# Two row blocks of the first norm's modulation sums weighted on ScalarE and added on TensorE

## The chip, the cores and the metric

The kernel runs on one core of one Trainium2 chip. TensorE multiplies matrices into PSUM, VectorE and ScalarE do element-wise work, GpSimd (POOL) helps, and DMA queues carry data from HBM to SBUF. The metric is device time in microseconds (us) of one execution, start to end, lower is better. Three unprofiled runs of the kernel before took 1736.28, 1736.1 and 1733.9 us, median 1736.1.

## The reference

Two transformer-like blocks on 512 tokens of width 1024. What bears on this change is the very start of the first block: a conditioning vector `c` is turned into six vectors of 1024, two of which (`sh1`, `sc1`) shift and scale the first normalised input, before the first projection.

```
mod = jax.nn.silu(c) @ w_ada[l] + b_ada[l]
sh1, sc1, g1, sh2, sc2, g2 = jnp.split(mod, 6, axis=-1)
h = rms_norm(x, g_mix_norm[l]) * (1.0 + sc1[:, None]) + sh1[:, None]
proj = h @ w_in[l]
q_lat, kv_lat, k_pe, qd, kd, vd = jnp.split(proj, SPLITS, axis=-1)
```

So no product with `w_in` can start before some columns of `sc1` and `sh1` are known, and these need 2048 columns of `w_ada` (8 MB in fp32), each a sum over 1024 rows.

## The kernel before, in words

All engines run programs of their own, written out by hand, and meet at semaphores; there is no scheduler. The order of instructions on an engine is the order in the code.

The first norm works in four rounds r = 0 to 3. A round gives the shift and scale of 256 of the 1024 features, which are two of the eight feature tiles k (128 features each) that the projection sums over. Its parts:

- SP loads `w_ada` in 16 blocks of 512 KB into `adab` (`ada_block`, L769), four to a round: block u = 4r + 2 half + kind, kind 0 the scale and 1 the shift columns, half the first or second four of the eight row blocks of 128 rows. Between them SP loads the first weights (`stage`, L714).
- VectorE forms `acol` = sum over the eight row blocks k of silu(c)[k] * w_ada block k, a tile of 128 partitions by 512 (2 kinds by 256 columns): `column(r, k)`, one multiplication (L2287) and seven multiply-adds (L2289, the last of them L2291, which counts up `acol_done`). `columns(r, k0, k1)` runs a stretch of them; two are placed early and six later.
- TensorE adds `acol` over its partitions in `block_sums(r)`: four fp32 matmuls (two records each in the trace, x8) of a 128x128 weight tile with one column of ones (L1616), into four columns of PSUM bank 4.
- VectorE's `modulation(r)` (L2303, L2305) turns them into `gsc` and `mod`.
- ScalarE's `z_first(r)` scales and shifts two tiles of x in PSUM into `zu` and `zhi` (L1022, L1024), VectorE takes the rest as `zlo` (`z_low_first`, L2351). `zhi` + `zlo` is a split of an fp32 number for two fast passes.
- TensorE's `scaled_turn(k)` (L1520) transposes x tile k and scales its rows, and `first_products(k, jobs)` (L1627) multiplies tile k with the first four weight tiles: three matmuls of 512 columns for each job. From L1484 on the later projections follow.
- The weights are split in the same way: ScalarE's `split_hi` (`whi`, L919) and VectorE's `split_lo` (`wlo`, L2214).

TensorE's order is: scaled_turn 0, 1; transposes of the parameters (L1532) and of the meta tokens (L1536); block_sums(0); scaled_turn(2); products of tiles 0 and 1 with jobs 0, 1; scaled_turn(3); block_sums(1); scaled_turn(4); products of tiles 0 and 1 with job 2; scaled_turn(5); block_sums(2); products of tiles 2 and 3 with jobs 0 to 2; scaled_turn 6, 7; products of tiles 0 to 3 with job 3; block_sums(3); the rest of the products.

Of the kernel before, what the change touches and what calls it, by code (L numbers as in the profile page):

```python
# [8 lines left out]
ACT = mybir.ActivationFunctionType  # L9
# [4 lines left out]
P = 128  # L14
D = 1024
KD = D // P
# [194 lines left out]
def emit(nc, A, out):  # L211
# [4 lines left out]
    with ctx:  # L216
        def sem(name):
            return ctx.enter_context(nc.semaphore(name))
# [5 lines left out]
        def at(name, shape, off, dt=F32):  # L224
            n = 4 * int(np.prod(shape[1:]))
            assert base + off + n <= end, (name, base + off + n - end)
            return nc.alloc_sbuf_tensor_at(name, shape, dt, offset=base + off)

        cst = at("cst", [P, NCONST], 0)
        o = 4 * NCONST  # L230
# [3 lines left out]
        csil = at("csil", [P, 8], o + 2368)  # L234
# [14 lines left out]
        SQO = o  # L249
# [18 lines left out]
        adab = at("adab", [P, NADA, 4, 256], FREE + 16384)  # L268
# [12 lines left out]
        TAB = LAT + 24576  # L281
        tab = at("tab", [P, 4, T1], TAB)
        acol = [at(f"acol{i}", [P, 2, 256], TAB + 8192 + 2048 * i) for i in range(2)]
        posi = at("posi", [P, T1], TAB + 12288, I32)
        posf = at("posf", [P, T1], TAB + 14336)
        angt = at("angt", [P, 2, T1], TAB + 8192)
# [81 lines left out]
        ps = ctx.enter_context(nc.psum_tensor("ps", [P, 8, 512], F32))  # L368

        def const(name, rows=P, n=P):  # L370
            return cst[0:rows, CONST[name]:CONST[name] + n]
# [35 lines left out]
        s_xin, s_cst, s_par, s_meta = sem("s_xin"), sem("s_cst"), sem("s_par"), sem("s_meta")  # L407
        bulk_in = [sem(f"bulk_in{i}") for i in range(8)]
        s_cst2, s_pos, s_c, acol_done = sem("s_cst2"), sem("s_pos"), sem("s_c"), sem("acol_done")
        act_setup, dve_setup = sem("act_setup"), sem("dve_setup")  # L410
        rows_in = sem("rows_in")
        wide_in = [s_cst, s_cst2]
        ring_in = [sem(f"ring_in{i}") for i in range(RING)]
# [4 lines left out]
        ada_done, mod_mm, conv_mid = sem("ada_done"), sem("mod_mm"), sem("conv_mid")  # L418
# [187 lines left out]
        SUM_STEPS = [t for t in range(HEADS // 2 * QB, NS) if t % QB >= 2]  # L606

        FIRST_BANK = (0, 2, 1, 3)
        XN_AT = (2, 3, 6, 7, 8, 9, 10, 11)

        def xn(k):
# [298 lines left out]
        def _(act):  # L910
            link = Chain(act, a_link)

            def split_hi(u, i=None, step=4):

                slot, value = plan.landed[plan.w_load[u]]
                act.wait_ge(landed[slot], plus(value, i, 16 * step // NST))
                if u >= NHL:
                    act.wait_ge(marks, plus(plan.free[u - NHL], i, step))
                act.activation(whi[u % NHL][:], stage[slot][:], ACT.Copy).then_inc(hi_done, 1)  # L919
# [58 lines left out]
            for name, src, k in PARAMS:  # L978
                flat = A[src].rearrange("a b c -> (a b c)" if len(A[src].shape) == 3 else
                                        "a b -> (a b)" if len(A[src].shape) == 2 else "a -> a")  # L980
                v, r0, done = flat.rearrange("(r c) -> r c", c=P), ROW[name], 0
# [4 lines left out]
                    done += m  # L986

            act.wait_ge(start_mm, 1)
            act.activation(csil[:, :], ps[:, 2, 0:KD], ACT.Silu).then_inc(act_setup, 1)
            act.wait_ge(pads, 1)  # L990
            act.wait_ge(s_xin, 16 * QB)
            for t in range(QB):
# [2 lines left out]
            for k in (6, 7):  # L995
                act.wait_ge(xt_done, 6)
                act.wait_ge(xt_mm, k + 1)
                act.activation(xT[:, k, META:T2], ps[:, 5 + k % 2, :], ACT.Copy).then_inc(xt_done, 1)
            split_hi(0)
            split_hi(1)  # L1000

# [12 lines left out]
            def z_first(r):  # L1014

                act.wait_ge(dve_setup, 4 + r)
                for k in (2 * r, 2 * r + 1):
                    if k < 6:
                        act.wait_ge(start_mm, XN_AT[k])
                        if k >= NZU:  # L1020
                            act.wait_ge(zlo_done, k - NZU + 1)
                        act.activation(zu[:, k % NZU, 0:T1], xn(k), ACT.Identity, scale=gsc[:, 0, k:k + 1],  # L1022
                                       bias=mod[:, k:k + 1])
                        act.activation(zhi[:, k, 0:T1], xn(k), ACT.Identity, scale=gsc[:, 0, k:k + 1],  # L1024
                                       bias=mod[:, k:k + 1]).then_inc(zhi_done, 1)
                    else:
                        act.wait_ge(zu_done, 4 * (k - 5))
                        act.activation(zhi[:, k, 0:T1], zu[:, k % NZU, 0:T1], ACT.Copy).then_inc(zhi_done, 1)

            z_first(0)  # L1030
            split_hi(2)
            z_first(1)
            split_hi(3)
            z_first(2)
            z_first(3)

            def raw(name, j, split=True):
# [377 lines left out]
            for j in range(8):  # L1415
                ahead("glu", j)
                if j % 2:
                    for h in (j - 1, j):
                        act.wait_ge(ostat_mm, h + 1)
                        act.activation(wide(KH[:, h, :], T2), ps[:, 4 + 2 * (h % 2):6 + 2 * (h % 2), 0:HT2], ACT.Ln,  # L1420
                                       scale=1.0 / P, bias=small[:, 0:1]).then_inc(oln_done, 1)
                n = J["glu"] + j
# [35 lines left out]
            for h in range(2):  # L1458
                act.wait_ge(stat_mm, STAT0[6] + h + 1)
                r = small[:, 48 + 2 * h:50 + 2 * h]  # L1460
# [10 lines left out]
        def _(pe):  # L1471
# [35 lines left out]
            for k in range(KD):  # L1507
                if k >= 2:
                    pe.wait_ge(xt_done, k - 1)
                for t in range(QB):  # L1510
                    mm = pe.transpose(ps[:, 5 + k % 2, t * P:(t + 1) * P], xrow[:, t, k * P:(k + 1) * P], const("ident"))
                mm.then_inc(xt_mm, 1)
            def scaled_turn(k):

                if k == 2:
                    pe.wait_ge(dve_setup, 3)
                elif k > 2:
                    pe.wait_ge(zhi_done, k - 2)
                for t in range(QB):
                    mm = pe.matmul(ps[:, 5 + k % 3, t * P:(t + 1) * P], xrow[:, t, k * P:(k + 1) * P], diag[:, t, :],  # L1520
                                   start=True, stop=True)
                mm.then_inc(start_mm, 1)

            pe.wait_ge(dve_setup, 1)
            pe.wait_ge(xt_done, KD)
            scaled_turn(0)
            scaled_turn(1)
            pe.wait_ge(s_par, 16 * n_par)
            pe.wait_ge(s_par2, 16 * n_par2)
            for b in range(NBLK):  # L1530
                r = min(P, NROWS - b * P)
                mm = pe.transpose(ps[:, 1, b * P:b * P + r], prow[0:r, b, :], const("ident", r, r))  # L1532
            mm.then_inc(start_mm, 1)
            pe.wait_ge(s_meta, 16)
            for k in range(KD):
                mm = pe.transpose(ps[:, 7, k * META:(k + 1) * META], metar[:, k * P:(k + 1) * P],  # L1536
                                  const("ident", META, META))
# [67 lines left out]
                            if (h, k) == (1, KD - 1):  # L1605
                                mm.then_inc(marks, 1)

            def block_sums(r):

                if r:  # L1610
                    pe.wait_ge(dve_setup, 3 + r)
                pe.wait_ge(acol_done, r + 1)
                for i in range(2):
                    for kind in range(2):
                        c = 4 * r + 2 * i + kind
                        mm = pe.matmul(ps[:, 4, c:c + 1], acol[r % 2][:, kind, i * P:(i + 1) * P],  # L1616
                                       const("ones", n=1), start=True, stop=True)
                mm.then_inc(mod_mm, 1)

            def first_products(k, jobs):  # L1620

                pe.wait_ge(zlo_done, k + 1)
                for j in jobs:
                    if k == 0:
                        pe.wait_ge(split_done, j + 1)
                    for a, x in ((whi, zhi), (whi, zlo), (wlo, zhi)):
                        mm = pe.matmul(ps[:, FIRST_BANK[j], :], a[j][:, k * P:(k + 1) * P], x[:, k, 0:T1],  # L1627
                                       start=(k == 0 and a is whi and x is zhi), stop=(k == KD - 1 and a is wlo))
                    if k == KD - 1:
                        mm.then_inc(marks, 1)  # L1630
# [2 lines left out]
            scaled_turn(2)  # L1633
            first_products(0, (0, 1))
            first_products(1, (0, 1))
            scaled_turn(3)
            block_sums(1)
            scaled_turn(4)
            first_products(0, (2,))
            first_products(1, (2,))  # L1640
            scaled_turn(5)
            block_sums(2)
            first_products(2, (0, 1, 2))
            first_products(3, (0, 1, 2))
# [1 line left out]
            scaled_turn(7)  # L1646
            for k in range(4):
                first_products(k, (3,))
            block_sums(3)
            for k in range(4, KD):  # L1650
                first_products(k, (0, 1, 2))
# [530 lines left out]
            for j in range(8):  # L2182
                gemm("glu", j, zx(zhi), zx(zlo), T2, fresh=(ylo_done, 0) if j == 0 else None)
                if j % 2 == 0:
                    for h in (j, j + 1):
# [7 lines left out]
                        for b, t0, t1 in halves(T2):  # L2193
                            mm = pe.matmul(ps[:, 4 + 2 * (h % 2) + b, 0:HT2], const("ones"), KH[:, h, t0:t1],
                                           start=True, stop=True)
# [12 lines left out]
        def _(dve):  # L2208
# [68 lines left out]
            def column(r, k):  # L2277

                u = 4 * r + 2 * (k // 4)
                o, w, c = acol[r % 2][:, :, :], adab[:, u:u + 2, k % 4, :], csil[:, k:k + 1]  # L2280
                if k % 4 == 0:
                    for v in (u, u + 1):
                        dve.wait_ge(bulk_in[v % 8], 16 * (v // 8 + 1))
                if k == 0:
                    if r >= 2:
                        dve.wait_ge(mod_mm, r - 1)
                    link(dve.tensor_scalar(o, w, c, None, ALU.mult))  # L2287
                elif k < KD - 1:
                    link(dve.scalar_tensor_tensor(out=o, in0=w, scalar=c, in1=o, op0=ALU.mult, op1=ALU.add))  # L2289
                else:  # L2290
                    dve.scalar_tensor_tensor(out=o, in0=w, scalar=c, in1=o, op0=ALU.mult, op1=ALU.add).then_inc(acol_done, 1)  # L2291
# [16 lines left out]
                    else:  # L2308
                        ins.then_inc(dve_setup, 1)

            dve.wait_ge(act_setup, 1)
            for k in range(6):
                dve.wait_ge(xt_mm, k + 1)
                dve.tensor_copy(xT[:, k, META:T2], ps[:, 5 + k % 2, :]).then_inc(xt_done, 1)
# [668 lines left out]
            for j in range(8):  # L2983
# [15 lines left out]
                n = J["sp"] + j  # L2999
# [268 lines left out]
```

## Time and profile before

| what | us |
|---|---|
| median of three runs | 1736.1 |
| the profiled execution | 1734.03 |
| its span, first to last instruction | 1732.2 |
| TensorE busy | 1682.1 (97%) |
| VectorE busy | 1100.9 (64%) |
| ScalarE busy | 748.2 (43%) |
| GpSimd busy | 301.2 (17%) |

The 1.8 us between the profiled execution's time and its span lie before the first and behind the last instruction. Busy time is the sum of an engine's instruction records. Matmul ends are modelled and overlap the next start, so starts of matmuls are the better measure of pace. PEclk is the granted share of TensorE's full clock: 1.00 is 2.4 GHz, 0.50 is 1.2 GHz. The first norm lies in the first 60 us of the span. In the kernel after, line numbers differ by 2 to 35.

### The profile page before, as it was taken

How to read it: one execution, taken by the hardware profiler on the slowest of the kernel's cores; microseconds unless marked ns; L12 is line 12 of the kernel's file. 1: busy time of each engine (PE TensorE's matmuls, PEld its weight loads, DVE VectorE, ACT ScalarE, POOL GpSimd, SP SyncE). 2: the span in 40 equal slices, each digit the busy share in tenths (PEclk: the TensorE clock that was granted, in tenths of full speed). 3: DMA queues.
4: the chain of work that ended last, by engine and by line, in shares of the span. 5: the costliest groups of instructions: out<-in, count | busy, mean ns of one | idle time of the engine just before them, and what ended most of it. 6: DMA issues, size and time to landing. Idle time of an engine off the chain costs nothing.

```text
span 1732.2 us, 32425 instructions
## 1 busy us (share of the span) xinstructions
PE 1682.1 (97%) x12801; PEld 1493.0 (86%) x12801; DVE 1100.9 (64%) x1761; ACT 748.2 (43%) x1115; POOL 301.2 (17%) x289
## 2 busy tenths in 40 slices
PE   5999999999999999899999999999999999999998
PEld 4776666888888888799999999999999999989986
DVE  6877586777764668855869663444653766655633
ACT  4479574555332342632323554356233643323313
POOL 2112395211000003441015221110102000000002
PEclk8999999999999999999999999999999999999999
DMA  9453632343333232264336952242532233232332
GB/s 314 124 141 103 183 111 89 107 115 103 99 96 98 85 97 75 88 166 133 119 107 171 226 135 94 82 130 86 167 111 86 74 97 98 87 101 80 97 97 74
DMA packets 320398, 201.17 MB, mean 116 GB/s; under 512 B 50511, under 2 KB 303046, under 8 KB 320150
## 3 DMA queue, kind: packets, MB, share of 16 engines
q1 hardware_dynamic: 300208, 160.79, 33.2%
q0 software_dynamic: 7952, 24.83, 4.7%
q10 hardware_dynamic: 12118, 13.88, 2.3%
q8 instruction: 85, 1.39, 0.3%
q14 instruction: 35, 0.29, 0.1%
HBM read 177.75 MB, written 17.24 MB: 113 GB/s over the span
## 4 chain that ended last, share of the span: by engine, by line
PE 80%; DVE 9%; ACT 5%; issue 2%; DMA 2%; SPq 1%; POOL 1%; ACTq 0%; DVEq 0%
PE ps L1484 66%; DVE wlo L2214 2%; PE ps L1799 1%; PE ps L1686 1%; PE ps L1809 1%; PE ps L1825 1%; ACT whi L919 1%; PE ps L1627 1%; DMA stage<-in_w_in_dram 1%; PE ps L1603 1%; DVE acol L2289 1%; PE ps L2057 1%; PE ps L2151 1%; DVE LF L2876 1%; DMA xrow<-in_x_dram 1%
## 5 line engine op out<-in xcount | busy, mean ns | idle before, releaser
L1484 PE MATMUL ps<-zhi,whi 128*128 128x258 f32 (+2 forms) x2072 | 638.1, 308 | 1.4 <-ACT ub L1217 0.6
L1484 PE MATMUL ps<-zlo,whi 128*128 128x258 f32 (+2 forms) x2072 | 633.5, 306 | 0.0
L1484 PE MATMUL ps<-zhi,wlo 128*128 128x258 f32 (+2 forms) x2072 | 632.1, 305 | 0.0
L1484 PEld LDWEIGHTS ps<-zhi,whi 128*128 128x128 f32 x2072 | 390.9, 189 | 27.1 <-issue 3.9
L2214 DVE TENSOR_TENSOR wlo<-stage,whi 128x1024 fp32r<-128x1024 f32 x256 | 329.4, 1288 | 126.9 <-ACT whi L919 114.9
L1484 PEld LDWEIGHTS ps<-zlo,whi 128*128 128x128 f32 x2072 | 390.1, 188 | 19.0 <-issue 0.5
L1484 PEld LDWEIGHTS ps<-zhi,wlo 128*128 128x128 f32 x2072 | 390.8, 189 | 18.0
L919 ACT ACTIVATE whi<-stage 128x1024 fp32r<-128x1024 f32 x256 | 269.3, 1054 | 293.2 <-PE ps L1484 242.0
L1484 PE MATMUL ps<-ghi,whi 128*128 128x512 f32 x340 | 134.7, 396 | 0.0
L1484 PE MATMUL ps<-glo,whi 128*128 128x512 f32 x340 | 134.3, 395 | 0.0
L1484 PE MATMUL ps<-ghi,wlo 128*128 128x512 f32 x340 | 134.0, 394 | 0.0
L1217 ACT ACTIVATE ub<-ps 128x512 f32<-128x512 f32 (+1 forms) x88 | 52.6, 598 | 163.0 <-PE ps L1484 161.7
L3101 POOL TENSOR_TENSOR zu<-zu,sq 128x528 f32<-128x528 f32 (+1 forms) x18 | 31.7, 1761 | 425.5 <-ACT sq L927 424.6
L2629 DVE TENSOR_SCALAR cv<-ub,par 128x512 f32<-128x512 f32 (+1 forms) x88 | 49.0, 557 | 70.4 <-ACT ub L1217 70.4
L1227 ACT ACTIVATE ghi<-cv 128x512 f32 (+1 forms) x44 | 27.9, 634 | 124.3 <-DVE cv L2644 124.3
L1484 PEld LDWEIGHTS ps<-ghi,wlo 128*128 128x128 f32 x340 | 64.0, 188 | 15.0
L1484 PEld LDWEIGHTS ps<-ghi,whi 128*128 128x128 f32 x340 | 63.9, 188 | 14.7
L1484 PEld LDWEIGHTS ps<-glo,whi 128*128 128x128 f32 x340 | 63.9, 188 | 14.6
L2545 DVE TENSOR_TENSOR xT<-ps,xT 128x512 f32 (+2 forms) x30 | 20.8, 692 | 85.1 <-PE ps L1484 85.1
L2638 DVE SCALAR_TENSOR_TENSOR cv<-ub,par,cv 128x512 f32<-128x512 f32 (+1 forms) x88 | 66.3, 754 | 13.1 <-DVE cv L2632 6.7
L3094 POOL TENSOR_SCALAR pb<-pb,small 128x128 f32<-128x128 f32 (+3 forms) x64 | 72.8, 1156 | 9.6 <-DVE small L2519 9.2
L1274 ACT ACTIVATE spill<-ps 128x516 f32<-128x516 f32 (+1 forms) x40 | 24.2, 604 | 102.3 <-PE ps L1484 102.2
(449 smaller groups left out, 2806.0 us busy)
## 6 DMA issues: line engine op xcount, KB each, us to landing
stage<-in_w_up_dram SPq DMA_DIRECT2D x88, 512.0 KB, 3.8
stage<-in_w_in_dram SPq DMA_DIRECT2D x74, 512.0 KB, 4.0
stage<-in_w_down_dram SPq DMA_DIRECT2D x32, 512.0 KB, 4.0
ring<-in_w_ada_dram POOLq DMA_DIRECT2D x24, 512.0 KB, 4.5
adab<-in_w_ada_dram SPq DMA_DIRECT2D x16, 512.0 KB, 7.9
stage<-in_w_down_dram SPq DMA_DIRECT2D x16, 384.0 KB, 3.4
stage<-in_w_o_dram SPq DMA_DIRECT2D x8, 512.0 KB, 4.1
ring<-in_w_ada_dram SPq DMA_DIRECT2D x8, 512.0 KB, 3.9
```

The source lines that it names most:

```text
L919: act.activation(whi[u % NHL][:], stage[slot][:], ACT.Copy).then_inc(hi_done, 1)
L1217: act.activation(wide(ub[:, j % 2, 2:2 + T], T), acc(job, T), ACT.Copy).then_inc(emptied[job % 2], 1)
L1227: act.activation(ghi[c % 2][:, bass.ds(i * 2 + q, 1), 0:T].rearrange("p a t -> p (a t)"), cv[:, q, 1, 0:T], ACT.Copy).then_inc(ghi_done, 1)
L1274: act.activation(wide(spill[m % 2][:, T2 - T:T2], T), acc(n, T), fn).then_inc(emptied[n % 2], 1)
L1484: last = pe.matmul(out, w(a, k), x(k, t0, t1), start=(k == 0 and a is whi and x is x_hi), stop=(k == ks - 1 and a is wlo))
L1603: mm = pe.matmul(o, a[(u + j) % NHL][:, k * P:(k + 1) * P], x[:, k, c], start=(k == 0 and a is whi and x is zhi), stop=(k == KD - 1 and a ...
L2214: dve.tensor_tensor(wlo[u % NHL][:], stage[plan.w_load[u] % NST][:], whi[u % NHL][:].bitcast(F32), ALU.subtract).then_inc(split_done, 1)
L2545: ins = dve.tensor_tensor(x, acc(job, T), x, ALU.add)
L2629: link(dve.tensor_scalar(o, ub[:, g, 2:2 + T], tap(2), par[:, bass.ds(i * 2 + (ROW[f["cb"]] + ft), 1)], ALU.mult, ALU.add))
L2638: dve.scalar_tensor_tensor(out=o, in0=ub[:, g, 0:T], scalar=tap(0), in1=o, op0=ALU.mult, op1=ALU.add).then_inc(conv_done, 1)
L3094: pool.tensor_scalar(pb[:, t % 4, r, 0:w], pb[:, t % 4, r, 0:w], total(t, r, 32), None, ALU.mult)\
L3101: pool.tensor_tensor(square(n, 0), square(n, 0), square(n, 1 + j % 2), ALU.add).then_inc(acc_done, 1)
```

## The change

In each round ScalarE takes over row blocks 3 and 7 (`APART`). It writes silu(c)[k] times the block into a tile of its own, `bcol` (one activation of 128x512 for each of the two blocks), and VectorE's `column` returns for these two. TensorE gets `apart_sums(r)`: for each of the four PSUM columns two matmuls, one for each of the two `bcol` tiles, eight in all, which open the accumulation; `block_sums(r)` then adds its four matmuls onto the same columns. `bcol` has two buffers, in memory that is free at that time. ScalarE's `apart(0)` stands behind its two copies of x, ahead of the first weight splits; the others stand behind `z_first(0)`, `split_hi(2)` and `z_first(2)`. `apart_sums(0)` stands behind scaled_turn(1), the others as below. The wait of `block_sums` for `dve_setup` goes to `apart_sums`.

```diff
+        bcol = [at(f"bcol{i}", [P, 2, 2, 256], o) for i, o in enumerate((SQO, TAB + 2048))]
+        APART = (3, KD - 1)
@@ ScalarE
+            def apart(r):
+                if r >= 2:
+                    act.wait_ge(mod_mm, r - 1)
+                for a, k in enumerate(APART):
+                    u = 4 * r + 2 * (k // 4)
+                    for v in (u, u + 1):
+                        act.wait_ge(bulk_in[v % 8], 16 * (v // 8 + 1))
+                    act.activation(bcol[r % 2][:, a, :, :], adab[:, u:u + 2, k % 4, :], ACT.Copy, scale=csil[:, k:k + 1])\
+                       .then_inc(cond_done, 1)
+            act.wait_ge(cond_done, 1)
+            apart(0)
             split_hi(0)
             split_hi(1)
...
             z_first(0)
+            apart(1)
             split_hi(2)
+            apart(2)
             z_first(1)
             split_hi(3)
             z_first(2)
+            apart(3)
             z_first(3)
@@ TensorE
+            def apart_sums(r):
+                if r:
+                    pe.wait_ge(dve_setup, 3 + r)
+                pe.wait_ge(cond_done, 2 * r + 3)
+                for i in range(2):
+                    for kind in range(2):
+                        for a in range(2):
+                            c = 4 * r + 2 * i + kind
+                            pe.matmul(ps[:, 4, c:c + 1], bcol[r % 2][:, a, kind, i * P:(i + 1) * P], const("ones", n=1),
+                                      start=i + kind + a == 0, stop=False, skip_group_check=True)
...
             scaled_turn(0)
             scaled_turn(1)
+            apart_sums(0)
...
             first_products(1, (0, 1))
+            apart_sums(1)
             scaled_turn(3)
             block_sums(1)
...
             scaled_turn(5)
+            apart_sums(2)
             block_sums(2)
...
+            apart_sums(3)
             block_sums(3)
@@ VectorE, column(r, k)
+                if k in APART:
+                    return
...
-                elif k < KD - 1:
+                elif k < KD - 2:
```

Three places show how the order moves. TensorE, start of the program: the transposes of the constants (`prow`, `metar`) and the first sums, before:

```order
L1520 MATMUL ps<-diag,xrow 128x128 x8
L1532 MATMUL ps<-cst,prow 128x128 x3
L1532 MATMUL ps<-cst,prow 128x85
L1536 MATMUL ps<-cst,metar 128x16 x8
L1616 MATMUL ps<-cst,acol_92 128x1 x4
```

and now:

```order
L1538 MATMUL ps<-diag,xrow 128x128 x8
L1551 MATMUL ps<-cst,bcol_94 128x1 x8
L1573 MATMUL ps<-cst,prow 128x128 x3
L1573 MATMUL ps<-cst,prow 128x85
L1577 MATMUL ps<-cst,metar 128x16 x8
L1560 MATMUL ps<-cst,acol_92 128x1 x4
```

The eight new matmuls stand ahead of both transposes. ScalarE, from its copies of x to the second pair of z tiles, now:

```order
L1000 ACTIVATE xT<-ps 128x512 x2
L1009 ACTIVATE bcol_94<-adab,csil 128x512 x2
L921 ACTIVATE whi_57<-stage_55 128x1024
L921 ACTIVATE whi_58<-stage_56 128x1024
L1037 ACTIVATE zu<-ps,mod,gsc 128x512
L1039 ACTIVATE zhi<-ps,mod,gsc 128x512
L1037 ACTIVATE zu<-ps,mod,gsc 128x512
L1039 ACTIVATE zhi<-ps,mod,gsc 128x512
L1009 ACTIVATE bcol_95<-adab,csil 128x512 x2
L921 ACTIVATE whi_59<-stage_55 128x1024
L1009 ACTIVATE bcol_94<-adab,csil 128x512 x2
```

The rows with `bcol` are the new ones; the others stand in the order of before. VectorE, the sums of round 0 around the diagonal tiles, before:

```order
L2289 SCALAR_TENSOR_TENSOR acol_92<-adab,csil,acol_92 128x512
L2318 RECIPROCAL small<-small 128x4
L2320 TENSOR_SCALAR diag<-cst,small 128x128 x4
L2289 SCALAR_TENSOR_TENSOR acol_92<-adab,csil,acol_92 128x512 x5
L2291 SCALAR_TENSOR_TENSOR acol_92<-adab,csil,acol_92 128x512
```

and now:

```order
L2323 SCALAR_TENSOR_TENSOR acol_92<-adab,csil,acol_92 128x512
L2352 RECIPROCAL small<-small 128x4
L2354 TENSOR_SCALAR diag<-cst,small 128x128 x4
L2323 SCALAR_TENSOR_TENSOR acol_92<-adab,csil,acol_92 128x512 x3
L2325 SCALAR_TENSOR_TENSOR acol_92<-adab,csil,acol_92 128x512
```

Both skipped row blocks belong to the later stretch of a round, which falls from six multiply-adds to four.

## Rows read from the trace of the kernel before

**Rows 1.** Page header and busy time: us, share of the span, instructions.
```profile
span 1732.2 us, 32425 instructions
PE 1682.1 (97%) x12801; PEld 1493.0 (86%) x12801; DVE 1100.9 (64%) x1761; ACT 748.2 (43%) x1115; POOL 301.2 (17%) x289
```

**Rows 2.** Windows: stretch, length, TensorE busy (records), granted clock, DMA share, GB/s.
```profile
28.00:46.70 18.70, 12.14 (x67) 0.82 1.07 368
46.70:63.50 16.80, 16.80 (x86) 1.00 0.31 97
63.50:100.00 36.50, 36.50 (x155) 1.00 0.46 120
100.00:150.00 50.00, 50.00 (x245) 1.00 0.56 134
```

**Rows 3.** TensorE timeline: start us, us, line, out<-in, records [idle before <-releaser].
```profile
20.95 3.12 PE L1520 MATMUL ps<-diag,xrow 128*128 128x128 f32 x16 [1.64 <-DVE diag L2320]
23.86 0.99 PE L1532 MATMUL ps<-cst,prow 128*128 128x128 f32 x4
24.77 0.80 PE L1536 MATMUL ps<-cst,metar 16*128 16x16 f32 x8
25.54 1.05 PE L1616 MATMUL ps<-cst,acol 128*128 128x1 f32 x8
31.95 0.80 PE L1627 MATMUL ps<-zhi,whi 128*128 128x512 f32 x1 [2.77 <-DVE zlo L2351]
32.53 0.63 PE L1627 MATMUL ps<-zlo,whi 128*128 128x512 f32 x1
32.96 0.63 PE L1627 MATMUL ps<-zhi,wlo 128*128 128x512 f32 x1
...
35.68 0.39 PE L1627 MATMUL ps<-zhi,whi 128*128 128x512 f32 x1
35.91 0.39 PE L1627 MATMUL ps<-zlo,whi 128*128 128x512 f32 x1
...
36.38 1.05 PE L1520 MATMUL ps<-diag,xrow 128*128 128x128 f32 x8
37.91 1.02 PE L1616 MATMUL ps<-cst,acol 128*128 128x1 f32 x8 [0.47 <-DVE acol L2291]
41.17 0.47 PE L1627 MATMUL ps<-zhi,whi 128*128 128x512 f32 x1 [1.24 <-DVE wlo L2214]
...
45.77 1.02 PE L1616 MATMUL ps<-cst,acol 128*128 128x1 f32 x8 [2.08 <-DVE acol L2291]
...
55.47 0.95 PE L1616 MATMUL ps<-cst,acol 128*128 128x1 f32 x8
56.28 0.48 PE L1627 MATMUL ps<-zhi,whi 128*128 128x512 f32 x1
```

**Rows 4.** VectorE timeline, same columns.
```profile
20.81 3.90 DVE L2289 SCALAR_TENSOR_TENSOR acol<-adab,csil,acol 128x512 f32<-128x512 f32 x5
24.74 0.75 DVE L2291 SCALAR_TENSOR_TENSOR acol<-adab,csil,acol 128x512 f32<-128x512 f32 x1
26.54 0.64 DVE L2325 COPY par<-ps 128x469 f32<-128x469 f32 x1
27.22 0.17 DVE L2327 TENSOR_SCALAR mod<-par 128x8 f32<-128x8 f32 x1
27.42 0.29 DVE L2329 COPY xT<-ps 128x128 f32<-128x128 f32 x1
27.63 1.22 DVE L2214 TENSOR_TENSOR wlo<-stage,whi 128x1024 fp32r<-128x1024 f32 x1
28.76 0.21 DVE L2303 SCALAR_TENSOR_TENSOR gsc<-ps,mod,par 128x1 f32<-128x1 f32 x1
...
39.04 0.22 DVE L2303 SCALAR_TENSOR_TENSOR gsc<-ps,mod,par 128x1 f32<-128x1 f32 x1
```

**Rows 5.** ScalarE timeline, same columns.
```profile
22.93 1.06 ACT L919 ACTIVATE whi<-stage 128x1024 fp32r<-128x1024 f32 x1 [2.93 <-DMA stage<-in_w_in_dram]
34.42 1.06 ACT L919 ACTIVATE whi<-stage 128x1024 fp32r<-128x1024 f32 x1 [1.98 <-DMA stage<-in_w_in_dram]
39.93 0.78 ACT L1022 ACTIVATE zu<-ps,mod,gsc 128x512 f32<-128x512 f32 x1 [4.46 <-PE ps L1520]
58.31 1.29 ACT L1028 ACTIVATE zhi<-zu 128x512 fp32r<-128x512 f32 x2 [6.59 <-DVE zu L2372]
```

**Rows 6.** Issues of `adab` blocks that touch 31 to 33 us: durations ns, starts.
```profile
L769 SPq DMA_DIRECT2D adab<-in_w_ada_dram x3: 730/1107/1276, 30.3 to 32.8; - x3
DMA to landing us min/median/max: 6.7/6.7/6.9
```

**Rows 7.** Windows: length, busy us of PE, PEld, DVE, ACT, POOL, granted clock, DMA, GB/s.
```profile
22.00:24.00 2.00, 2.00 (x11) 2.00 (x11) 1.89 (x4) 1.06 (x1) 0.00 (x0) 0.50 0.77 217
26.00:28.00 2.00, 0.83 (x8) 0.74 (x8) 1.93 (x5) 0.00 (x0) 0.00 (x0) 1.00 0.87 244
30.00:32.00 2.00, 0.06 (x1) 0.06 (x1) 1.47 (x3) 2.00 (x4) 0.00 (x0) 0.50 1.10 374
34.00:35.00 1.00, 1.00 (x4) 0.81 (x3) 0.96 (x2) 0.58 (x1) 0.00 (x0) 0.50 1.09 384
35.00:36.00 1.00, 1.00 (x5) 0.78 (x5) 0.96 (x2) 0.47 (x1) 0.00 (x0) 0.82 1.09 386
36.00:37.00 1.00, 1.00 (x9) 0.91 (x8) 0.94 (x2) 0.00 (x0) 0.00 (x0) 1.00 1.09 385
```

More of the change, by code:

```diff
@@ L409, in emit @@
         s_cst2, s_pos, s_c, acol_done = sem("s_cst2"), sem("s_pos"), sem("s_c"), sem("acol_done")
-        act_setup, dve_setup = sem("act_setup"), sem("dve_setup")
+        cond_done, dve_setup = sem("cond_done"), sem("dve_setup")
         rows_in = sem("rows_in")
@@ L988, in _ @@
             act.wait_ge(start_mm, 1)
-            act.activation(csil[:, :], ps[:, 2, 0:KD], ACT.Silu).then_inc(act_setup, 1)
+            act.activation(csil[:, :], ps[:, 2, 0:KD], ACT.Silu).then_inc(cond_done, 1)
             act.wait_ge(pads, 1)
@@ L1522, in scaled_turn, with block_sums @@
                 mm.then_inc(start_mm, 1)
+            def apart_sums(r):
[8 more added lines that the diff above has]
+                                      start=i + kind + a == 0, stop=False, skip_group_check=True)
+            def block_sums(r):
+                pe.wait_ge(acol_done, r + 1)
+                for i in range(2):
+                    for kind in range(2):
+                        c = 4 * r + 2 * i + kind
+                        mm = pe.matmul(ps[:, 4, c:c + 1], acol[r % 2][:, kind, i * P:(i + 1) * P],
+                                       const("ones", n=1), start=False, stop=True, skip_group_check=True)
+                mm.then_inc(mod_mm, 1)
             pe.wait_ge(dve_setup, 1)
@@ L1606, in first_pair @@
                                 mm.then_inc(marks, 1)
[L1608 to L1618, printed above, removed]
             def first_products(k, jobs):
@@ L2309, in modulation @@
                         ins.then_inc(dve_setup, 1)
-            dve.wait_ge(act_setup, 1)
+            dve.wait_ge(cond_done, 1)
             for k in range(6):
```

## The prediction, made before the changed kernel ran

> **What bounds the kernel now.** I read four views in this order: busy times, windows, the timelines of TensorE and VectorE in the first 60 us, and ScalarE's timeline beside them. The busy times make TensorE the bound, with 97% against VectorE's 64% and ScalarE's 43% [rows 1]. The windows say where it is not: from 28.0 to 46.7 us it works 12.14 of 18.7 us, and from 46.7 to 150 us it has no gap at all (16.80 of 16.80, 36.50 of 36.50, 50.00 of 50.00) [rows 2]. So in the first norm something else sets the pace up to 46.7 us, and from there every matmul added in front of or into the stream moves everything behind it by its own length. The later loads wait for work that TensorE releases, so I take the shift to reach the end whole.
>
> TensorE's timeline names its waits in the three rounds that the change wants to shorten: 2.77 us before the first product (for `zlo`), 0.47 before block_sums(1), 1.24 before the products of job 2 (for `wlo`), 2.08 before block_sums(2); before block_sums(3) there is none [rows 3]. Only 0.47 and 2.08 are waits for `acol`, which is what the change shortens. This is the number to hold on to: 2.55 us, while VectorE is busy with `acol` nearly the whole time.
>
> **What is removed.** Two of eight row blocks leave VectorE: five multiply-adds take 3.90 us with their gaps [rows 4], 0.78 each, so 1.56 us a round, 6.2 in four. In round 3 TensorE does not wait for `acol`, so that part is hidden already. In round 0 the six later blocks end with `acol` at 25.49 (24.74 + 0.75), but modulation(0) starts only at 28.76, behind wlo, the parameter copy, the meta copy and a second wlo on VectorE [rows 4].
>
> **What is added on ScalarE.** Eight activations of 128x512 from SBUF. The nearest row is `zhi<-zu`, 1.29 us for two [rows 5]; the 0.78 of the rows that read PSUM is the upper end. So 1.3 to 1.6 us a round. They lie in waits: apart(0) in the 2.93 before the first `whi`, apart(1) in the 1.98 before the third (0.4 to 0.7 left), apart(2) in the 4.46 before z_first(1), apart(3) in the 6.59 before z_first(3) [rows 5]. apart(2) needs the four blocks of round 2; the last of them was issued at 30.3 and took 6.7, landing at 37.0 [rows 6]; z_first(1) starts at 39.93 before and at about 41.3 after, and 37.0 + 1.3 = 38.3 is in front of both. I cost ScalarE at nothing; without that cover, a round would be 1.3 later.
>
> **What is added on TensorE.** Eight fp32 matmuls of one column a round. The four of block_sums(3) stand in a dense stretch: 55.47 to the next start at 56.28, 0.81 us, 0.20 each [rows 3]. Eight are 1.62. The bounds from rows: the eight 16-column transposes of `metar` take 0.77 together (24.77 to 25.54), and eight scaled-turn matmuls at half clock 2.91 (20.95 to 23.86) [rows 3]. I take 1.62, the same form at the same clock.
> A word on this price. The row says 0.20 us for a matmul of one column, which is two records of 0.10. The Trainium skill (TensorE: Matmul & The Clock Gate, Back-to-back issue gap) gives a floor near 25 ns from start to start for 1 to 64 columns; by that rule the eight would take about 0.4 us (an estimate) and the sum below would come out near -1.0. The same page (LDWEIGHTS) has a load of 128 weight columns at about 107 ns, and every one of these matmuls has weights of its own. The trace, with 0.10 a record, agrees with the second and not with the first.
>
> **The sum, as the shift of TensorE against before.**
> - Round 0. The eight stand at 23.86, where the clock is at half (0.50 from 22 to 24) and full by 26 [rows 7]: I take 2.1 us, between 1.62 and 2.91. The two sets of transposes behind them (23.86 to 25.54, 1.68) then end at 27.64, which before was 25.54. VectorE's meta copy, at 27.42 before, now waits until about 27.8; behind it are wlo and modulation(0) [rows 4]. The modulation starts about 0.4 later (nothing to 1.2). The freed 1.56 us of VectorE is lost in front of that copy. The first product moves from 31.95 to 32.35. In the trace it runs at half clock up to some time between 35 and 36 (0.82 there), 0.43 a matmul against 0.23 behind it [rows 3, 7]. If the clock rises at the same time, half of the 0.4 comes back: **+0.2**.
> - Round 1. TensorE reaches block_sums(1) after the products, the eight and scaled_turn(3): +1.62, and the wait of 0.47 goes, since `acol` is ready 1.2 earlier than before (+0.4 - 1.56): **+1.62 - 0.47**. Shift so far 1.35, and modulation(1), z_first(1) and split_lo(2), which follow it, are later by as much. The 1.24 before job 2 stays: `wlo` moves along.
> - Round 2. +1.62 and -2.08: **-0.46**. `acol` would be ready at 45.77 + 1.35 - 1.56 = 45.56, TensorE at 45.77 - 2.08 + 1.35 + 1.62 = 46.66, so TensorE is late now, not `acol`. Shift 0.89.
> - Round 3. No wait to win: **+1.62**. Shift 2.51.
>
> Sum: 0.2 + 3 x 1.62 - 2.55 = 2.5 us later. Behind that nothing new is late: modulation(3) follows block_sums(3) as before, and so do z tiles 6 and 7. The profiled execution, 1734.03 (span 1732.2 and 1.8 around it), would become 1736.5. The median of the three runs stands 2.1 above it and would become 1738.6. Two of the four executions known lie near 1736.2 and two near 1734; their mean is 1735.1. I take a base halfway between mean and median, 1735.6, and predict **1738.1**.
>
> **The rivals.**
> - *The matmuls are cheap (faster).* One mechanism: a one-column matmul behind another costs less than in block_sums. The shift is 0.2 - 2.55 + 3m for a price m of eight, so it turns below m = 0.78, just at the 0.77 of the `metar` row. At m = 0 VectorE takes over as the bound in round 2, since a round of it is only 1.56 shorter: 0.2 - 0.47 - 1.56 = -1.8 us. So between -1.8 and 0, 1734.7 at the middle. For it: VectorE is what TensorE waits for twice. Against: the four L1616 rows show 0.95 to 1.05 for four, and the dense one 0.81 from start to start [rows 3]. 9%. Even free, this change gives no more than 0.1%.
> - *The clock comes up later.* The first products start later and the rise at 35 to 36 us is missed. Then twelve products cost 5.2 instead of 4.2 us and the next eight up to 2.91 instead of 1.62: +2.3, in all 4.8, 1740.4. For it: the first products open the busy stretch 0.4 later. Against: TensorE is otherwise busier than before. 12%.
> - *The clock is up earlier.* The new sums fill a part of 26 to 28 us, where TensorE works 0.83 of 2 us; were the clock full at 32, eight products would save 0.2 each: -1.6, in all 0.9, 1736.5. Against: it has 0.50 with TensorE idle from 30 to 32 [rows 7], and that wait for `zlo` stays. The Trainium skill (TensorE: Matmul & The Clock Gate, Loop structure matters more than you think) has the same: dense work keeps the clock, a wait loses it. The trace agrees. 11%.
> - *ScalarE's tiles are late.* A block of round 2 that lands 4 us later than in rows 6 holds z_first(1), and with it scaled_turn(5): about +2 more, 1740. 4%.
> - *The shift is absorbed.* Some later stage waits for a thing that TensorE does not release; then 0, 1735.6. Against: no gap up to 150 us. 4%.
>
> **How the numbers follow.** The forecast has 60%, its own range +1.5 to +3.5, 1737.1 to 1739.1. The range takes in both clock cases and the price bounds above 0.77: 0 to +4.8 on 1735.6, widened by 0.6 for the base: 1735.0 to 1741.0. What a measurement can tell from no change is about 0.2%, 3.5 us. The clock-late case and most of late tiles lie above, 15%; of the forecast I give 9%, since the base itself is known to 1 to 2 us. That makes slower 0.24. Faster by 3.5 us is out of reach of the mechanism, 0.04 for a base that was high. The same: 0.72.
>
> **What would show it.** In the trace after: 16 records in 1.6 us in each of rounds 1 to 3 for the new sums; no wait before block_sums(1) and (2); the meta copy on VectorE waiting for TensorE near 27 us; modulation(1) near 40.4 instead of 39.04 [rows 4]; VectorE idle before it by 2 us; the products behind block_sums(3) starting at 58.8 instead of 56.28 and the gapless stretch as long as before. If that start is at 56 or earlier, the price of the eight or the round-0 term is wrong; if it is at 58.8 and the end does not move, the step that carries the shift to the end is wrong.

## The result, and the profile after

The changed kernel is slower: 1743.59 us median of six runs (1740.32 to 1745.66) against 1735.49 of before, ratio 1.0044, 95% interval 1.0034 to 1.0054. Six further runs, beside a median of before of 1735.46, gave 1742.03, ratio 1.0035 (1.0023 to 1.0047). The forecast was 1738.1, about 2.5 us slower; measured are 8.1 and 6.6. The direction was right, the size was not.

The head of the profile after, to set beside [rows 1]:

```profile
span 1743.9 us, 32561 instructions
PE 1695.1 (97%) x12865; PEld 1503.5 (86%) x12865; DVE 1095.2 (63%) x1753; ACT 753.4 (43%) x1123; POOL 301.2 (17%) x289
```

TensorE has 64 records more, which is 4 rounds of 8 matmuls of 2 records. Its busy time grew by 13.0 us, though the 32 matmuls are worth about 7 (32 x 0.21, the 0.21 from the rows below). So other instructions became longer. TensorE's timeline in the changed kernel, to set beside [rows 3] (start us, us, line, out<-in, records):

```profile
20.77 2.05 PE L1538 MATMUL ps<-diag,xrow 128*128 128x128 f32 x16 [1.65 <-DVE diag L2354]
22.66 1.84 PE L1551 MATMUL ps<-cst,bcol 128*128 128x1 f32 x16
24.37 0.60 PE L1573 MATMUL ps<-cst,prow 128*128 128x128 f32 x4
...
36.12 2.20 PE L1551 MATMUL ps<-cst,bcol 128*128 128x1 f32 x16
38.18 1.14 PE L1538 MATMUL ps<-diag,xrow 128*128 128x128 f32 x8
39.16 0.95 PE L1560 MATMUL ps<-cst,acol 128*128 128x1 f32 x8
...
45.05 1.91 PE L1538 MATMUL ps<-diag,xrow 128*128 128x128 f32 x8
46.75 2.02 PE L1551 MATMUL ps<-cst,bcol 128*128 128x1 f32 x16
48.63 1.03 PE L1560 MATMUL ps<-cst,acol 128*128 128x1 f32 x8
...
59.90 1.84 PE L1551 MATMUL ps<-cst,bcol 128*128 128x1 f32 x16
61.60 1.03 PE L1560 MATMUL ps<-cst,acol 128*128 128x1 f32 x8
```

Both waits for `acol` are gone (no bracket behind L1560). The eight new matmuls take 1.71 us from start to start in round 0 (22.66 to 24.37) and 1.70 in round 3 (59.90 to 61.60), where the clock is full, but 2.06 in round 1 (36.12 to 38.18), which begins at half clock, and 1.88 in round 2 (46.75 to 48.63). And scaled_turn(5), 45.05 to 46.75, takes 1.70 instead of 0.9 us. The windows say why (stretch, length, TensorE busy, granted clock, DMA share, GB/s), beside [rows 2, 7]:

```profile
27.00:36.00 9.00, 6.90 (x20) 0.50 1.05 347
37.00:40.00 3.00, 3.00 (x29) 1.00 1.10 371
41.00:47.00 6.00, 5.39 (x20) 0.50 1.02 368
51.00:53.00 2.00, 2.00 (x6) 0.50 0.03 7
54.00:60.00 6.00, 6.00 (x37) 1.00 0.19 56
```

Before, the clock rose at 35 to 36 us and stayed up to 150 us. Now it is at half up to 36 us and full from 37, falls behind the sums of round 1 (36 to 40 us) and again behind those of round 2 (46.75 to 49.5), while TensorE works without a gap from 42.35 on. VectorE waits for it (start us, us, line, idle before), beside [rows 4]:

```profile
40.22 0.22 DVE L2337 SCALAR_TENSOR_TENSOR gsc<-ps,mod,par 128x1 f32<-128x1 f32 x1 [3.96 <-PE ps L1560]
49.77 0.22 DVE L2337 SCALAR_TENSOR_TENSOR gsc<-ps,mod,par 128x1 f32<-128x1 f32 x1 [2.16 <-PE ps L1560]
62.67 0.22 DVE L2337 SCALAR_TENSOR_TENSOR gsc<-ps,mod,par 128x1 f32<-128x1 f32 x1 [6.69 <-PE ps L1560]
```

The relief of VectorE is now its idle time: 3.96, 2.16 and 6.69 us. Before, it had no such wait in rounds 1 and 2 and one of 0.62 us in round 3.

### The profile page after: what moved, and what is told of

Read it like the earlier page. It is cut to its first block, busy times and chain, and to the rows that moved or that the text cites. A ratio compares the mean times of both kernels' runs of the same rounds, so it can differ in the third digit from the quotient of the medians.

```text
span 1743.9 us, 32561 instructions
## 1 busy us (share of the span) xinstructions
PE 1695.1 (97%) x12865; PEld 1503.5 (86%) x12865; DVE 1095.2 (63%) x1753; ACT 753.4 (43%) x1123; POOL 301.2 (17%) x289
## 4 chain that ended last, share of the span: by engine, by line
PE 85%; DVE 6%; ACT 4%; issue 2%; DMA 1%; POOL 1%; SPq 0%; ACTq 0%; DVEq 0%; POOLq 0%
PE ps L1502 69%; PE ps L1656 2%; DVE wlo L2246 1%; DMA stage<-in_w_in_dram 1%; PE ps L1831 1%; PE ps L1718 1%; PE ps L1841 1%; PE ps L1857 1%; PE ps L1644 1%; PE ps L2089 1%; ACT whi L921 1%; PE ps L2183 1%; DVE LF L2910 1%; PE ps L1738 1%; PE ps L2066 1%
```

## The experiments

Each version was timed beside the kernel before, whose median was 1735.2 to 1735.7 us each time; the ratios are the safest comparison between versions.

Theory 1, **clock**: rounds of twelve one-column matmuls lose the clock, and the half-clock stretches are what the forecast lacks. Theory 2, **work**: it is the length of the added matmuls and a wait further back.

**All sums with 128 columns of ones** (more work, one thing changed; VectorE reads one column of each result):

```
-  c = 4 * r + 2 * i + kind
-  pe.matmul(ps[:, 4, c:c + 1], bcol[...], const("ones", n=1), ...)
+  c = P * (2 * i + kind)
+  pe.matmul(ps[:, 4, c:c + P], bcol[...], const("ones"), ...)      # acol's sums likewise
```

> The changed kernel with every sum of the four rounds (the eight new and the four old matmuls) taken with 128 columns of ones instead of one; one column of each result is read. Theory 1, clock: what went beyond the forecast is TensorE at half clock, because the twelve one-column matmuls of a round do not keep the clock up. With 128 columns the granted clock stays at 1.00 from about 36 us on, although each matmul costs 0.24 instead of 0.20 us (12 x 0.04 = 0.5 us a round more): 1737 to 1740, ratio 1.001 to 1.0025. Theory 2, work: the loss is the length of the added matmuls and what it displaces later. Then it gets 2 us worse than the changed kernel, about 1745.5, ratio 1.0055, and the clock falls at 40 us as before.

Measured: 1736.5 us, ratio 1.0006 (0.9997 to 1.0015). Its windows from 37 to 100 us (with the busy times of all engines between length and clock), and its eight of round 2 (the last row is the first record of the next sums; the view ends there):

```profile
37.00:62.00 25.00, 23.65 (x159) 21.31 (x158) 16.01 (x31) 9.81 (x15) 1.09 (x2) 1.00 0.57 184
62.00:100.00 38.00, 38.00 (x162) 30.21 (x161) 29.96 (x38) 23.78 (x34) 7.59 (x6) 1.00 0.42 118
```
```profile
43.76 1.05 PE L1538 MATMUL ps<-diag,xrow 128*128 128x128 f32 x8
44.65 1.95 PE L1551 MATMUL ps<-cst,bcol 128*128 128x128 f32 x16
46.44 0.28 PE L1560 MATMUL ps<-cst,acol 128*128 128x128 f32 x1
```

The clock is full in both windows, the eight take 1.79 us instead of 1.71, and the kernel is 5.5 to 7.1 us faster than with one column. Theory 2 expected it to be slower.

**TensorE's matmuls alone**, on the kernel before (constants as weights, nobody reads the result), once with one column and once with 128 in these and in block_sums. The second has one thing more: its new matmuls wait for VectorE to have read the sums of the round before, since they write over them. The first:

```
+  for i in range(8):     # in the four places of the new sums
+      pe.matmul(ps[:, 4, 16 + i:17 + i], const(("ident", "ones")[i % 2]), const("ones", n=1), start=True, stop=True)
```

> The kernel before with eight further one-column fp32 matmuls of constants in each round, in the four places of the new sums; VectorE and ScalarE as before. Theory 1 (clock): the full loss comes from TensorE's new instructions, through length and clock, and VectorE's relief gave back little: ratio 1.004 to 1.007, with stretches at half clock behind 38 us. Theory 2 (work): 4 x 1.62 less the waits that they fill, about +4 us, ratio 1.002 to 1.003, clock as before.

> The kernel before with eight further fp32 matmuls of constants in each round, in the places of the new sums, as in the run with one column (1742.6), but these and the four of block_sums with 128 columns of ones; VectorE and ScalarE as before. Clock theory: with the clock held only length counts: rounds 1 to 3 add 3 x 1.8 and fill waits of 0.5 and 2.1, about +3, 1738 to 1739, ratio 1.0015 to 1.0025, no half clock behind 38 us. Rival (the loss is in the number of instructions, not in the columns): 1742 or more.

Measured: 1742.59, ratio 1.0039 (1.0026 to 1.0053) with one column; 1739.05, ratio 1.0017 (1.0009 to 1.0026) with 128. Windows of the first, and of the second:

```profile
43.00:46.00 3.00, 3.00 (x12) 0.50 1.04 389
50.00:52.00 2.00, 2.00 (x7) 0.50 0.00 0
64.00:66.00 2.00, 2.00 (x6) 0.50 0.96 342
```
```profile
37.00:62.00 25.00, 23.36 (x157) 1.00 0.53 174
```

VectorE and ScalarE do the work of before in both, so the loss is TensorE's, and half of it (3.9 of 7.4 us) goes with the columns. What is left with 128 columns, 3.5 us, is the length that the clock theory expected (about 3).

**The relief of VectorE alone**: the changed kernel without `apart_sums`. Two of the eight row blocks are missing from the sums.

> The changed kernel without the eight new matmuls a round: the two row blocks are weighted by ScalarE and left out of the sums. This is the relief of VectorE alone. Both theories: between -1.0 and -3 us, ratio 0.9985 to 0.9995, TensorE's waits for acol gone or below 0.6 us. If it comes to 0.996 or less, VectorE's relief was worth more than the waits that the trace of before named.

Measured: 1731.38, ratio 0.9979 (0.997 to 0.9988). What is left of the wait for `acol` (us in total, times, longest):

```profile
PE ps L1563 <- DVE acol L2324: 0.5, 1, 0.5
```

The relief is worth 3.8 us in the times (2 to 5 by the interval), more than the 1 to 3 that was expected here and the 1.8 that the prediction had as its most. The profile shows 2.3 of it: VectorE's copy of the positions, which hangs on the first product job, starts at 64.4 instead of 66.7 us. The wait before block_sums(1) is gone and the one of 2.08 us is down to 0.5. The rest is not in the two profiles at all, whose spans differ by 2.1 us (1730.1 and 1732.2): the profiled execution of before, 1734.03, lies 1.1 below the median of its runs here (1735.16), and the one of this version, 1731.91, lies 0.5 above its own. What makes executions of one kernel differ by that much was not traced.

**ScalarE alone**: its eight activations into tiles that nobody reads, VectorE as before, TensorE too but for a wait for these tiles ahead of block_sums.

> The kernel before with ScalarE's eight activations and their waits, whose tiles nobody reads; VectorE sums all eight row blocks, TensorE as before. Both theories: no change, ratio 0.9995 to 1.0005. A third theory, that the activations or their waits for blocks of the conditioning weights hold up the first norm: ratio 1.001 or more, with z_first later in the trace.

Measured: 1736.03, ratio 1.0002 (0.9993 to 1.0011). They cost nothing that can be measured, to within 2 us. Its profile has something else: one half-clock stretch behind 38 us, though TensorE's work is that of before, with four one-column sums in the round. It begins 2 us after these sums start, and they stand behind a wait of 2.07 us for `acol`:

```profile
46.43 1.02 PE L1563 MATMUL ps<-cst,acol 128*128 128x1 f32 x8 [2.07 <-DVE acol L2322]
49.00:51.00 2.00, 2.00 (x6) 1.55 (x5) 1.93 (x5) 1.40 (x3) 0.00 (x0) 0.50 0.00 0
```

**128 columns in the kernel before**:

> The kernel before with 128 columns of ones in block_sums, nothing else changed. It costs 4 x 0.04 us a round, 0.6 us in all. Theory 1 (clock): the four one-column sums of before seldom lose the clock, so the time is the same to 1.5 us faster, ratio 0.999 to 1.0003, and its runs lie closer together. Theory 2: 0.6 slower, ratio 1.0003 to 1.0005.

Measured: 1734.98, ratio 0.9998 (0.9989 to 1.0006). Inconclusive on speed, and the runs (1733.25 to 1736.5) lie no closer together than most of before: four one-column sums a round cost nothing that the times show, though the profile of ScalarE alone has a stretch behind them.

**The changed kernel a second time**:

> The changed kernel once more, for a second profile. If the wait of 2.7 us for rtp near 145 us belongs to the change, it stands in this profile too; if it comes from how the small weight loads landed in that execution, it is below 1 us here. Theory 1: stretches at half clock between 38 and 66 us again, at other places, 1740 to 1745. Theory 2: none, and the time is near the forecast of 1738.

Measured: 1742.03, as above. The question was a wait for `rtp`, a tile that VectorE writes for the stage near 150 us: TensorE waits 2.7 us for it in the first profile of the changed kernel, and stands at half clock behind it (0.51 from 146 to 153 us), against a wait of 0.8 us before. Windows of the second profile, and the waits for `rtp` in the first and in the second:

```profile
37.00:42.00 5.00, 3.76 (x33) 1.00 1.09 358
43.00:45.00 2.00, 2.00 (x9) 0.50 1.05 373
46.00:49.00 3.00, 3.00 (x27) 1.00 0.49 155
50.00:52.00 2.00, 2.00 (x6) 0.50 0.07 12
53.00:62.00 9.00, 9.00 (x62) 1.00 0.10 30
63.00:66.00 3.00, 3.00 (x9) 0.50 0.92 300
```
```profile
PE ps L1756 <- DVE rtp L2444: 2.7, 1, 2.7
PE ps L1752 <- DVE rtp L2444: 0.9, 1, 0.9
```

Three stretches, one behind each of rounds 1 to 3, at other times than in the first profile. The 2.7 us wait for `rtp` and the half clock behind it were that execution's; they are not the change's.

**The new sums apart from block_sums**, one column: those of round 1 between tiles 0 and 1, of round 2 behind scaled_turn(4), of round 3 behind scaled_turn(7).

> The changed kernel, all sums with one column, but the eight new matmuls of rounds 1 to 3 stand apart from the four of block_sums: those of round 1 between the products of tiles 0 and 1, of round 2 behind scaled_turn(4) in the wait for wlo, of round 3 behind scaled_turn(7), 2.9 us of products ahead of block_sums(3). Work is the same. Clock theory, as the experiments left it: what loses the clock is twelve one-column matmuls close together; apart, fewer or none of the half-clock stretches behind 38 us remain, each worth 1.7 us: 1735.5 to 1739, ratio 1.0005 to 1.002. Rival (each one-column matmul costs the clock wherever it stands): three stretches remain and only the 1.2 us of the wlo wait is won, 1740 to 1742.

Measured: 1741.39, ratio 1.0038 (1.0023 to 1.0053), runs from 1737.12 to 1748.22. The expectation of the clock theory was missed. The profile is that of the fastest run and has one stretch, behind the eight of round 3 and ahead of block_sums(3):

```profile
36.00:55.00 19.00, 18.67 (x130) 1.00 0.71 238
56.00:58.00 2.00, 2.00 (x6) 0.50 0.00 0
60.00:67.00 7.00, 7.00 (x31) 1.00 0.46 150
```

So the twelve need not stand in one piece; here the clock fell behind eight, which stood behind two scaled turns. Spacing of this kind did not help in the times.

**128 columns, rounds 0 to 2 only**:

> The version with 128 columns of ones in all sums, the change made in rounds 0 to 2 only; round 3 as before. With the clock held, TensorE's length is what is left: round 3 has no wait that the relief of VectorE could shorten, so leaving it out wins its eight matmuls, 8 x 0.24 = 1.9 us: 1734.6 against 1736.5. If round 3 costs nothing because it is made up later, 1736.5.

Measured: 1737.34, ratio 1.0008 (1.0 to 1.0017), against 1.0006 for the version with all four rounds. This too was missed. In the profiles the 2.1 us are there early: VectorE's copy of the positions starts in the version with four rounds and in this one at

```profile
L2460 DVE CAST posf<-posi x1: 1527/1527/1527, 69.1 to 69.1; 128x512 f32<-128x512 int32 x1
```
```profile
L2460 DVE CAST posf<-posi x1: 1521/1521/1521, 67.0 to 67.0; 128x512 f32<-128x512 int32 x1
```

yet the spans are 1733.6 and 1733.8. The lead is lost in waits further back. TensorE's waits for `rtp` near 154 us and for `Vt`, a tile of ScalarE's, at 890 us, here:

```profile
PE ps L2089 <- ACT Vt L1300: 1.3, 1, 1.3
PE ps L1752 <- DVE rtp L2444: 1.1, 1, 1.1
```

With all four rounds it waits 0.3 us for `rtp` and not at all for `Vt`; before, 0.8 and 0.7. Together with a third wait at 1022 us (0.65 against 0.27) that is 2.4 us, so the 2.1 are accounted for in this pair of profiles. Why `Vt` is ready later here was not traced.

**A version that beats both.** GpSimd, idle there, adds ScalarE's two tiles, so TensorE has four new matmuls a round; rounds 0 to 2 only; those of round 0 stand behind the transposes. With 128 columns, with one, and the first once more:

```
+  for r in range(3):                                   # GpSimd
+      pool.wait_ge(cond_done, 2 * r + 3)
+      pool.tensor_tensor(bcol[r % 2][:, 0, :, :], bcol[r % 2][:, 0, :, :], bcol[r % 2][:, 1, :, :], ALU.add)
...
-  for a in range(2):                                   # TensorE
+  for a in range(1):
```

> The changed kernel, but GpSimd adds ScalarE's two tiles into one, so that TensorE has four new matmuls a round instead of eight; only in rounds 0 to 2 (round 3 is as in the kernel before); the four of round 0 stand behind the transposes; all sums take 128 columns of ones. Theory 1 (clock): the relief of VectorE measured without the sums, 3.8 us, less 4 x 0.24 in two rounds, of which 0.5 fills what is left of the acol wait: about -2.4, 1732 to 1734, ratio 0.998 to 0.9995, clock at 1.00 behind 38 us. Theory 2 (work and GpSimd's time): the new hop over GpSimd is late and the sums wait for it: 1736 or more.

> The same kernel with one column of ones in all sums. Theory 1 (clock): although every matmul is 0.04 us shorter, it is slower than the version with 128 columns, by 1 to 4 us, ratio 0.9995 to 1.002, with stretches at half clock between 38 and 60 us. Theory 2: faster than that version by 12 x 0.04 and more, 0.5 to 1 us.

> The fastest version so far (GpSimd adds ScalarE's two tiles, four new matmuls in rounds 0 to 2, all sums with 128 columns) once more, on whatever chip comes. If its gain of 2.3 us holds: ratio 0.998 to 0.9995, and the interval of both calls together clear of 1. If it was the draw of the runs: ratio 0.9995 to 1.0005.

Measured: 1733.14, ratio 0.9988 (0.9979 to 0.9996); one column 1733.9, ratio 0.999 (0.9981 to 0.9999); again 1733.81, ratio 0.9992 (0.9983 to 1.0). By the ratios 1.4 to 2.1 us faster than before and some 7.5 to 10 faster than the changed kernel. Each interval only just stays clear of 1 or touches it, but all three medians lie on the same side. Up to four things differ from the changed kernel at once (GpSimd's additions with half the matmuls, the rounds, the place in round 0, the columns); which of them is worth what was not separated. GpSimd's additions in the first (duration ns, starts), and the clock of the one-column version:

```profile
L3112 POOL TENSOR_TENSOR bcol<-bcol x3: 1262/1267/1277, 20.8 to 37.8; 128x512 f32<-128x512 f32 x3
```
```profile
36.00:62.00 26.00, 24.76 (x149) 1.00 0.64 213
```

The hop takes 1.27 us and is over before TensorE asks for it (no wait of TensorE for GpSimd in these stages). That 128 columns would be better than one was expected and is wrong here: with four to eight one-column matmuls a round the clock stayed in this profile, and the two are alike.

## Why the prediction was wrong in size

The starts of four places on TensorE, as the shift against before in us (31.95, 37.91, 45.77 and 56.28 there), beside the forecast:

| place | forecast | changed, first profile | changed, second | all sums with 128 columns |
|---|---|---|---|---|
| first product | +0.4 | -1.1 | -0.9 | -1.2 |
| block_sums(1) | +1.35 | +1.25 | +0.8 | +1.1 |
| block_sums(2) | +0.9 | +2.9 | +1.8 | +0.7 |
| products behind block_sums(3) | +2.5 | +6.2 | +5.15 | +2.35 |

Its last line, where the prediction had 58.8, from the three profiles:

```profile
62.49 0.48 PE L1656 MATMUL ps<-zhi,whi 128*128 128x512 f32 x1
61.43 0.48 PE L1656 MATMUL ps<-zhi,whi 128*128 128x512 f32 x1
58.63 0.48 PE L1656 MATMUL ps<-zhi,whi 128*128 128x512 f32 x1
```

- *The step that failed*: "+1.62" in rounds 2 and 3, the eight counted by their own length alone, with the clock at full for everything behind 36 us. Round 2 was to give -0.46 and gave +1.6 and +1.0; round 3 was to give +1.62 and gave +3.4 in both profiles. With 128 columns, where the clock held, they gave -0.4 and +1.7. In the half-clock stretches products cost 0.43 instead of 0.23 us, and the clock fell two to three times behind the sums. The missing term is 3.9 and 4.4 us at VectorE's copy of the positions (73.0 and 73.5 against 69.1 us), and 5.5 to 7.1 in the times; in the first profile the wait for `rtp` adds to it.
- *TensorE's price, 1.62 a round*: right where the clock is full, 1.71 and 1.70; 2.06 and 1.88 in rounds 1 and 2 of the first profile. The floor of 25 ns of the Trainium skill (TensorE: Matmul & The Clock Gate, Back-to-back issue gap) is not what such a matmul costs when each has its own weights: 0.107 us a record. The prediction's estimate by that floor, "near -1.0", comes to -1.15 from its own terms.
- *Rounds 0 and 1*: the waits are gone and TensorE is late in place of `acol`, as forecast, and modulation(1) stands at 40.22, forecast 40.4. That this number fits is luck: two errors cancel. Round 0 was to be +0.2 and the first product came 1.1 early. There was no half-clock stretch at the scaled turns (20.77 to 22.66, 1.89 us instead of 2.91 in [rows 3]), and the meta copy on VectorE stood at 26.31, without a wait, where one near 27 was forecast. Round 1 was to add 1.15 and added 2.4: the twelve products took 5.28 us (30.84 to 36.12) instead of 4.43, all at half clock, and the eight 2.06. The clock at these places differs from execution to execution. The version with 128 columns shows the same pair of errors (-1.2, then +2.3).
- *The rival "the clock comes up later"*, 12%, was partly there in the first profile: the clock rose between 36 and 37 us instead of 35 to 36. It cost some 1.2 us there (5.28 for 4.43 and 2.06 for 1.71), not 2.3, and the earlier start took that back. (It has twelve products at 4.2 us before; [rows 3] give 4.43, 31.95 to 36.38.) It looked only at when the clock rises, and excluded a fall by "TensorE is otherwise busier than before". Busier by the records it was.
- *ScalarE at nothing*: right (1.0002), though the last block of round 2 landed at 38.0 and not 37.0.
- *The shift reaches the end*: not whole. With 128 columns it is +2.4 at the copy (69.1 against 66.7) and 1.4 in the span: the waits for `rtp` (0.8 to 0.3) and `Vt` (0.7 to none) take up 1.1 of it. So the rival "the shift is absorbed", 4%, holds for a part, and the prediction looked for gaps only up to 150 us. In the second profile of the changed kernel it is 6.8 (73.5) and 6.9. The version with 128 columns is the forecast's kernel as it was reckoned, with the clock held: +2.5 forecast, +2.4 at that copy, 1.0006 (0.9997 to 1.0015) in the times.
- *What VectorE's relief gives*: 3.8 us by itself (2.3 of it seen in the profile), which the prediction bounded at 1.8. It did not decide: TensorE's sums fill the same waits that the relief removes. On the kernel before they cost 7.4 us, and with the relief still 6.6 to 8.1.

Shown: where eight more of these matmuls stand in a round, the columns decide (two pairs of kernels), and the loss is TensorE's. The half-clock stretches that began between 38 and 100 us, by profile: two, three, three and one in the four profiles of kernels with twelve one-column matmuls a round; none, none, none and one (ScalarE alone) in the four with four to eight; none in the six with 128 columns. Not shown: what it is about the one-column matmuls that loses the clock, how many of them it takes (the one stretch behind four came behind a wait of 2.07 us as well), where between one and 128 columns it turns, and why the spaced version is no better.

## What to carry to other kernels

A matmul with one moving column and weights of its own was hardly cheaper here than one with 128 (1.71 against 1.79 us for eight), and many of them cost the clock of what stood behind them: look at the granted clock around such work, not only at whether the engine is busy. When helpers are added to relieve one engine, ask which engine reduces their results; an idle third engine can add the partial tiles first. If a stall of 2.5 us is the whole prize, price the replacement against it before moving work.

## What was not expected of the hardware

- The granted clock fell from 1.00 to 0.50 while TensorE had no gap: in the second profile of the changed kernel TensorE is busy 3.00 of 3.00 us from 46 to 49 and 9.00 of 9.00 from 53 to 62, and stands at 0.50 right behind both. The last wait of TensorE's in front of them is the 1.24 us before 41.9. What it had just done were, among products, twelve fp32 matmuls of one column, each with 128x128 weights of its own. The Trainium skill (TensorE: Matmul & The Clock Gate, Loop structure matters more than you think) has waits as what loses the clock and dense work as what keeps it; here dense instruction records were not enough. In the six profiles of kernels whose sums have 128 columns it stayed at 1.00 from 38 to 67 us.
- A 128-column fp32 matmul with its own weights is only 5% dearer than a one-column one (1.79 against 1.71 us for eight), so the wider form is nearly free. It paid in the two pairs with twelve a round (1.0006 against 1.0044, 1.0017 against 1.0039) and made no difference in the two with four to eight (0.9998 against before, 0.9988 against 0.999).
